# Mixture-of-experts rounds in a four-layer trunk: seven narrow rounds of 96 slots become alternating rounds of 96 and 64 slots, experts ranked by their token count

## What is computed

```python
def moe_ffn(h, router, w_gu, w_down):
    logits = (h @ router).astype(jnp.float32)
    top_v, top_i = lax.top_k(logits, TOP_K)                 # TOP_K = 2 of N_EXPERTS = 8
    w = jax.nn.softmax(top_v, axis=-1)
    combine = jnp.sum(jax.nn.one_hot(top_i, N_EXPERTS, dtype=jnp.float32) * w[..., None], axis=-2)
    gu = jnp.einsum('btd,edf->btef', h, w_gu)               # D_MODEL 1024 -> 2 * 1408
    g, u = jnp.split(gu, 2, axis=-1)
    act = jax.nn.silu(g) * u * combine[..., None].astype(h.dtype)
    return jnp.einsum('btef,efd->btd', act, w_down)         # 1408 -> 1024
```

## Time and profile before

| | us |
|---|---|
| median of three runs | 2552.91 (2550.69 to 2554.35) |
| the profiled execution, its own time | 2551.02 |
| its span, first to last instruction | 2549.2 |
| expert rounds of layer 1 in the trace | 808.8 to 1241.3 |
| expert rounds of layer 3 in the trace | 2092.3 to 2524.5 |

### The profile page before, as it was taken

How to read it: one execution, slowest core, us unless ns; L and a number is a source line. 1 busy time by engine, 2 the same in 40 slices (tenths; PEclk the granted TensorE clock), 3 DMA queues, 4 the chain that set the end, 5 groups by cost and what they waited for, 6 DMA issues and landing times.

```text
span 2549.2 us, 47861 instructions
## 1 busy us (share of the span) xinstructions
PE 2350.7 (92%) x21433; PEld 1688.1 (66%) x21433; DVE 477.5 (19%) x1366; ACT 400.2 (16%) x853; POOL 67.1 (3%) x111
## 2 busy tenths in 40 slices
PE   5998999999999999999798599999989899999997
PEld 3865667888887555445474478888868674555454
DVE  1324332000214000000202310002334331000001
ACT  1122232000101000000203320002133410000000
POOL 5000000000000000000100000000000000000000
PEclk7999999999999999999899589999989989999998
DMA  9758887543354999996668085413420069899971
GB/s 312 227 214 352 319 308 204 168 147 108 117 190 152 326 326 345 349 344 221 190 248 293 7 247 174 124 52 121 159 67 11 11 228 341 313 338 346 348 273 42
DMA packets 356876, 551.68 MB, mean 216 GB/s; under 512 B 11392, under 2 KB 311936, under 8 KB 344240
## 3 DMA queue, kind: packets, MB, share of 16 engines
q1 hardware_dynamic: 344208, 525.30, 59.4%
q0 software_dynamic: 5840, 17.72, 2.6%
q10 hardware_dynamic: 6688, 6.57, 0.8%
HBM read 537.24 MB, written 16.37 MB: 217 GB/s over the span
## 4 chain that ended last, share of the span: by engine, by line
PE 87%; DVE 5%; ACT 4%; DMA 3%; issue 1%; ACTq 0%; POOL 0%; SPq 0%; DVEq 0%; POOLq 0%
PE ps L626 84%; DMA ring<-in_ada_w 2%; ACT ring L1298 2%; ACT work L1298 1%; PE ps L1093 1%; PE ps L996 0%; DVE ring L1812 0%; DMA work<-y_rows,work 0%; DVE ring L1794 0%; DVE work L1675 0%; DVE ring L1817 0%; DVE ring L1947 0%; DVE ring L1802 0%; ACT hT L1298 0%; DMA y_rows<-work 0%
## 5 line engine op out<-in xcount | busy, mean ns | idle before, releaser
L626 PE MATMUL ps<-ring,work 128*32 128x256 f32 (+5 forms) x9576 | 790.4, 430 | 35.6 <-ACT work L1298 27.9
L626 PE MATMUL ps<-hT,ring 128*128 128x256 f32 x3200 | 706.0, 381 | 2.4 <-ACT hT L1298 2.1
L626 PEld LDWEIGHTS ps<-hT,ring 128*128 128x128 f32 x3200 | 608.0, 191 | 97.6 <-ACT work L1298 6.9
L626 PEld LDWEIGHTS ps<-ring,work 128*32 128x32 f32 (+2 forms) x9576 | 400.7, 114 | 400.5 <-issue 238.5
L1298 ACT ACTIVATE work<-ps 128x256 f32<-128x256 f32 (+4 forms) x276 | 115.0, 432 | 1475.8 <-PE ps L626 1280.6
L626 PE MATMUL ps<-work,ring 128*128 128x256 f32 (+1 forms) x1344 | 292.0, 377 | 10.5 <-DVE work L1879 5.9
L626 PEld LDWEIGHTS ps<-work,ring 128*128 128x128 f32 (+1 forms) x1344 | 244.6, 189 | 49.0 <-DVE work L1879 9.1
L626 PE MATMUL ps<-ring 64*64 64x64 f32 (+1 forms) x4192 | 185.0, 230 | 17.4 <-ACT ring L1298 7.2
L626 PEld LDWEIGHTS ps<-ring 64*64 64x64 f32 x4192 | 162.5, 139 | 57.0 <-ACT ring L1298 24.2
L1298 ACT ACTIVATE ring<-ps 128x512 f32<-128x512 f32 (+3 forms) x224 | 106.8, 483 | 349.4 <-PE ps L626 313.0
L626 PE MATMUL ps<-ring,csil 128*2 128x512 f32 x768 | 99.1, 606 | 20.1 <-DMA ring<-in_ada_w 19.8
(11 more groups left out here) (247 smaller groups left out, 990.8 us busy)
## 6 DMA issues: line engine op xcount, KB each, us to landing
ring<-in_moe_w_gu SPq DMA_DIRECT2D x96, 1536.0 KB, 9.7
ring<-in_ada_w SPq DMA_DIRECT2D x96, 1024.0 KB, 7.7
ring<-in_moe_w_down SPq DMA_DIRECT2D x48, 1536.0 KB, 11.0
ring<-in_ff_w_gu SPq DMA_DIRECT2D x88, 512.0 KB, 5.7
ring<-in_dn_w_in SPq DMA_DIRECT2D x32, 1024.0 KB, 5.5
ring<-in_moe_w_gu SPq DMA_DIRECT2D x32, 1024.0 KB, 5.5
ring<-in_ff_w_down SPq DMA_DIRECT2D x44, 512.0 KB, 6.9
ring<-in_moe_w_down SPq DMA_DIRECT2D x32, 512.0 KB, 6.2
```

What stands on the lines that cost most here:

```text
L626: return pe.matmul(out, lhsT, rhs, start=start, stop=stop, **kw)
```

## The change

Experts 1 to 7 are now sorted by their count on the chip. The three emptiest get rounds 1, 3 and 5, the next three rounds 2, 4 and 6, the fullest the wide round. Rounds 1, 3 and 5 have 64 slots and a body of their own, `small`, on PE, ACT and DVE. It pairs two blocks of 32 slots with two weight pieces: for one slice of the contraction the four tiles do block 0 and 1 of piece A and block 0 and 1 of piece B. Its gate and up part has 4 column sets of 8 groups, its down part 11 groups of four matmuls of 512 columns. There are two turns instead of three. The loop goes by twos, `small` and then `body`. Before a load into pieces 2 and 3 SP waits for the first down count as well. The count of 64 replaces 96 in the test for extra rounds of the experts in rounds 1, 3 and 5. At the start, `y_rows` is filled from slot 64 instead of 96 on for these three rounds. The core of the diff:

```diff
-CAP, BLK, GW, DW = 96, 32, 384, 256
+CAP, SMALL_CAP, BLK, GW, DW = 96, 64, 32, 384, 256
+ROUND_CAP = [CAP, SMALL_CAP, CAP, SMALL_CAP, CAP, SMALL_CAP, CAP] + [P] * (1 + EXTRA + 1)
...
@@ SP
                             if j in GU_FREE:
                                 sp.wait_ge(moe["p_gu"], (done[0] + r) * 6 + GU_FREE[j])
+                                if j in (GATE_D, UP_D):
+                                    sp.wait_ge(moe["p_dn"], (done[0] + r) * 4 + 1)
...
@@ POOL
-                r0 = CAP if x < NARROW else 0
+                r0 = ROUND_CAP[x] if x < NARROW else 0
                 po.dma_start(y_rows[P * x + r0:P * (x + 1), :], a["x_prompt"][0, r0:P]).then_inc(filled, 16)
...
@@ PE
+                def columns_small(q, pieces, bank, done):
+                    for j, _ in pieces:
+                        landed(q, j)
+                    for k in range(KC):
+                        for x, (j, width) in enumerate(pieces):
+                            for b in range(2):
+                                t = 2 * x + b
+                                ins = mm(ps[BLK * t:BLK * (t + 1), bank, 0:width], xg[:, k, BLK * b:BLK * (b + 1)],
+                                         weights(j, width)[:, k, :], k == 0, k == KC - 1)
+                    ins.then_inc(moe["p_gu"], done)
...
+                def down_small(q, s):
+                    pe.wait_ge(moe["a_at"], q * 3 + (1 + 2 * s))
+                    if s == 0:
+                        pe.wait_ge(moe["a_y"], q)
+                        pe.wait_ge(moe["d_y"], q)
+                        for j in (8, 9):
+                            landed(q, j)
+                    else:
+                        landed(q, 10)
+                    for c in (range(6, 11) if s else range(6)):
+                        w, n = down_rows(c), c - 6 * s
+                        for b in range(2):
+                            at = P * (n % 3) + 64 * (n // 3) + BLK * b
+                            for x in range(2):
+                                t = 2 * x + b
+                                ins = mm(ps[BLK * t:BLK * (t + 1), 4 + x, :], ma_T[:, s, at:at + BLK],
+                                         w[:, 512 * x:512 * x + 512], c == 0, c == 10, skip_group_check=True)
+                        if c in (2, 4, 7, 10):
+                            ins.then_inc(moe["p_dn"], 1)
+
+                def small(q):
+                    pe.wait_ge(moe["a_xg"], q + (i + 1))
+                    pe.wait_ge(moe["d_xg"], q + (i + 1))
+                    columns_small(q, ((GATE[0], GW), (GATE[1], GW)), PG[0], 1)
+                    columns_small(q, ((UP[0], GW), (UP[1], GW)), PU[0], 3)
+                    columns_small(q, ((GATE[2], GW), (GATE_D, DW)), PG[1], 1)
+                    columns_small(q, ((UP[2], GW), (UP_D, DW)), PU[1], 1)
+                    turn_small(q, 0)
+                    down_small(q, 0)
+                    pe.wait_ge(moe["d_act"], q * 3 + 3)
+                    pe.wait_ge(moe["d_g"], q + (i + 2))
+                    gather(0)
+                    gather(1)
+                    turn_small(q, 1)
+                    down_small(q, 1)
...
-                with pe.Fori(1, NARROW) as r:
-                    body(q0 + r, False)
+                with pe.Fori(1, NARROW, 2) as r:
+                    small(q0 + r)
+                    body(q0 + r + 1, False)
...
@@ DVE, overflow
-                link(dve.tensor_reduce(top_e, taken[:, 1:NE], AX.X, ALU.max))
...
+                link(tt(before_e[:, 0, :, 1:NE], taken[:, 0:NE, None].to_broadcast([P, NE, NARROW]),
+                        taken[:, None, 1:NE].to_broadcast([P, NE, NARROW]), ALU.is_gt))
+                link(dve.tensor_reduce(rank, before_e[:, 0, :, 1:NE], AX.X, ALU.add))
...
+                link(ts(where[:, 0:NE], rank, 2.0, 1.0, ALU.mult, ALU.add))
```

More of the change, by code:

```diff
@@ L235, in trunk @@
         raw, cand, where, taken = wk(8872, 2, NE), wk(8888, 2, CAND), wk(8936, CAND), wk(8960, CAND)
-        count, top_e, cap_e, is_top = wk(8984, NE), wk(8992, 1), wk(8993, NE), wk(9001, NE)
-        comb_c = wk(9009, 2, CAND)
+        count, cap_e, rank, high = wk(8984, NE), wk(8992, NE), wk(9060, NE), wk(9068, 2, NE)
+        comb_c = wk(9010, 2, CAND)
         iota = wk(9600, P)
@@ new lines, in turn_small @@
+                def turn_small(q, s):
+                    pe.wait_ge(moe["d_act"], q * 3 + (1 + 2 * s))
+                    if s == 1:
+                        pe.wait_ge(moe["a_at"], q * 3 + 1)
+                    for c in range(2 if s else 3):
+                        ins = pe.transpose(ps[:, 6, c * P:(c + 1) * P], ma_s[:, s, c * P:(c + 1) * P], ident)
+                    if s == 1:
+                        ins = pe.transpose(ps[:, 6, 2 * P:2 * P + 64], ma_s[0:64, s, 2 * P:3 * P], ident[0:64, 0:64])
+                    ins.then_inc(moe["p_tr"], 1 + s)
@@ L1523, in store, with output_small, store_small, small @@
                             .then_inc(moe["y_out"], 16)
+                def output_small(q):
+                    act.wait_ge(moe["p_dn"], q * 4 + 4)
+                    act.wait_ge(moe["y_out"], q * 64 + 64)
+                    f(y_m[0:64, :], ps[0:64, 4, :], ACT.Copy).then_inc(moe["a_y"], 1)
+                def store_small(q, r):
+                    act.wait_ge(moe["a_y"], q + 1)
+                    act.wait_ge(moe["d_y"], q + 1)
+                    for x in range(4):
+                        act.dma_start(y_rows[bass.ds(r * P, 64), QUARTER * x:QUARTER * (x + 1)],
+                                      y_m[64 * (x // 2):64 * (x // 2) + 64, QUARTER * (x % 2):QUARTER * (x % 2 + 1)]) \
+                            .then_inc(moe["y_out"], 16)
+                def small(r):
+                    q = q0 + r
+                    output(q - 1)
+                    act.wait_ge(moe["p_gu"], q * 6 + 1)
+                    act.wait_ge(moe["d_act"], q * 3)
+                    f(mg_s, ps[:, PG[0], 0:GW], ACT.Silu).then_inc(moe["a_silu"], 1)
+                    store(q - 1, r - 1)
+                    act.wait_ge(moe["p_gu"], q * 6 + 5)
+                    act.wait_ge(moe["d_act"], q * 3 + 1)
+                    f(mg_s[0:64, DW:GW], ps[0:64, PG[1], DW:GW], ACT.Silu)
+                    f(mg_s[:, 0:DW], ps[:, PG[1], 0:DW], ACT.Silu).then_inc(moe["a_silu"], 2)
+                    act.wait_ge(moe["p_tr"], q * 3 + 1)
+                    act.wait_ge(moe["p_dn"], q * 4)
+                    f(ma_T[:, 0, :], ps[:, 6, 0:GW], ACT.Copy).then_inc(moe["a_at"], 1)
+                    tokens(q + 1)
+                    act.wait_ge(moe["p_tr"], q * 3 + 3)
+                    f(ma_T[:, 1, 0:2 * P + 64], ps[:, 6, 0:2 * P + 64], ACT.Copy).then_inc(moe["a_at"], 2)
                 def body(r, first):
@@ L1578, in experts @@
                 body(0, True)
-                with act.Fori(1, NARROW) as r:
-                    body(r, False)
+                with act.Fori(1, NARROW, 2) as r:
+                    small(r)
+                    body(r + 1, False)
                 output(q0 + NARROW - 1)
@@ L2007, in overflow @@
                 link(stt(taken[:, 0:NE], count, float(NE), es, ALU.mult, ALU.subtract))
-                link(dve.tensor_reduce(top_e, taken[:, 1:NE], AX.X, ALU.max))
[L2009 to L2018, removed]
+                link(tt(before_e[:, 0, :, 1:NE], taken[:, 0:NE, None].to_broadcast([P, NE, NARROW]),
+                        taken[:, None, 1:NE].to_broadcast([P, NE, NARROW]), ALU.is_gt))
+                link(dve.tensor_reduce(rank, before_e[:, 0, :, 1:NE], AX.X, ALU.add))
+                ts(high[:, 0], rank, 2.5, None, ALU.is_gt)
+                ts(high[:, 1], rank, 5.5, None, ALU.is_gt)
+                link(ts(where[:, 0:NE], rank, 2.0, 1.0, ALU.mult, ALU.add))
+                link(stt(where[:, 0:NE], high[:, 0], -5.0, where[:, 0:NE], ALU.mult, ALU.add))
+                link(tt(where[:, 0:NE], where[:, 0:NE], high[:, 1], ALU.subtract))
+                link(tt(cap_e, high[:, 0], high[:, 1], ALU.add))
+                link(ts(cap_e, cap_e, float(CAP - SMALL_CAP), float(SMALL_CAP), ALU.mult, ALU.add))
+                dve.memset(where[:, 0:1], 0.0)
+                link(dve.memset(cap_e[:, 0:1], float(CAP)))
                 link(tt(count, count, cap_e, ALU.subtract))
@@ L2059, in chosen_rows @@
             def chosen_rows(l):
[L2061 to L2064, removed]
+                ts(col_v, slotv, -0.5, None, ALU.is_gt)
+                link(tt(col_w, slotv, cst[:, None, C_RCAP:C_RCAP + COLS].to_broadcast([P, 2, COLS]), ALU.is_lt))
                 link(tt(col_w, col_w, col_v, ALU.mult))
@@ L2131, in gated, with output_small, small @@
                     tt(ma_s[:, s, 0:DW], mg_s[:, 0:DW], ps[:, PU[s], 0:DW], ALU.mult).then_inc(moe["d_act"], 1)
+                def output_small(q):
+                    dve.wait_ge(moe["p_dn"], q * 4 + 4)
+                    dve.wait_ge(moe["y_out"], q * 64 + 64)
+                    cp(y_m[64:P, :], ps[64:P, 5, :]).then_inc(moe["d_y"], 1)
+                def small(r):
```

(18 more changed lines are left out.)

15 lines of the change are left out of this document (9 added, 6 removed).

## The result

The changed kernel takes 2506.1 us (median of 4 runs, 2505.7 to 2512.2) against 2552.7 (4 runs): a ratio of 0.9827, 95% interval 0.9812 to 0.9842. That is 46.6 us faster, where 84.5 were forecast, and 12 us above the range.

The account below looks back on a forecast made before the run. TensorE was taken to bound the kernel, DMA close behind. -96.6 (small rounds) + 2 x (4.0 wait + 1.5 clock) + 1.1 (fill) = -84.5 us, giving a forecast of 2468 us, range 2460 to 2478.

Parts of the forecast that it names:

- What bounds it: Expert rounds: TensorE bounds them, a narrow round needing 52.5 us of TensorE and 46.4 us of DMA.
- The price of a small round: Rounds 1, 3 and 5: each takes 36.4 us of TensorE, 16.1 us less than a narrow round.
- the 0.858 from the wide round: Small round's down part: a group of four tiles with 512 columns costs 0.858 us, the wide round's price per matmul.
- The step that failed: Three small rounds in each of two layers: 96.6 us less in all, if weights never come late.
- the rivals: Other outcomes: DMA binds harder 0.19, no wait 0.12, overlap worse 0.08, clock falls 0.06, a round more 0.02.
- something unseen: Chance left for the gain being lost in something the prediction did not see: 0.01.
- The waits for weights: Head of round 6: TensorE waits 4.0 us a layer for piece 2; no wait in rounds 1 to 5.
- The price of a piece: Weight loads: each of an expert's 11 pieces takes 4.22 us of DMA.
- The clock: After the wait for weights: half of a 3 us clock dip, 1.5 us more a layer.
- The fill of `y_rows`: At the start: the fill grows by 3 x 128 KB, 1.1 us more.
- The count of rounds: Rounds stay eight, one wide round a layer; the rival of a further round had chance 0.02, 2588 us.

Follow-up runs that it names:

- 1396: Instructions in TensorE's loop in the kernel before the change, which took 2552.7 us.
- 1552: Changed kernel with the small body in all of rounds 1 to 6, two in each pass of TensorE's loop: 2449.9 us.
- 1692: Changed kernel with slices 1 to 5 of each gate and up product left out in the looped narrow bodies: 2450.1 us.
- 1884: Changed kernel with slices 1 to 3 of each gate and up product left out in the looped narrow bodies: 2457.1 us.
- 1788: Changed kernel with slices 1 to 4 of each gate and up product left out in the looped narrow bodies: 2455.2 us.

## Why the prediction was wrong

- **What bounds it, right.** TensorE did, with DMA 6 us a narrow round behind, and some 3 us slower than TensorE in a pair with a small round (92.1 against 88.9).
- **The price of a small round, right.** In layer 1 a pair of small and narrow rounds takes 88.9 us (857.84 to 946.77, from one start of the last down part to the next but one); less the narrow round's 52.5 that is 36.4, as forecast. The six down slices of four tiles with 512 columns stand as 5.36 us, 0.89 each with the start of the stretch, so the 0.858 from the wide round was a fair price. 96.6 us of TensorE's work did go.
- **The step that failed** is the sentence under that sum, that three small rounds in each of two layers are 96.6 us less, if weights never come late. It made late weights the only way to lose them. The loop by twos was in my own list of what changes, and I priced its products and waits but not the jump back. TensorE's loop became larger than what is held near the engine, and each of the four jumps costs 11.7 to 12.5 us: gaps, and a low clock after them. It was none of the rivals; I had left 0.01 for something unseen. The trace of before could not show it, as nothing in it jumps back over so much code. The Trainium skill could have: "Runtime: NRT & Kernel Launch", under "Instruction fetch mechanics", says that a taken branch whose target isn't in the current window of two pages forces a fetch of the target page before execution can go on. That such a fetch stops the engine, the runs agree with. The sizes they don't bear out. Two pages of 256 instructions would have stopped the loops of 1396 and 1552 too. The 2048 instructions that the section gives TensorE would have held those of 1692 to 1884, where here the limit was near 1700.
- **The waits for weights, right, but hidden.** In the changed kernel none appears, because the gaps give the loads 24 us a layer to catch up. Without the gaps they are there, 6.1 us a layer where 4.0 were worked out: 4.1 at the head of round 6 for 4.0, and 2.0 at round 4, where I had none. The price of a piece was 4.19 us for 4.22.
- **The clock, right in size by luck** for a wait of 4 us. I had taken half of the dip in the earlier trace rows and called the whole one 3 us. But its 3 us at the low level are not lost whole: by the windows there the dip costs 2 x (0.02 + 0.50 + 0.34) = 1.7 us. After the wait of 4.12 us the whole dip came, 2.5 x (0.32 + 0.36) = 1.7 us, and after the waits of 2.0 and 1.8 us none. After the gaps it cost more, 2.5 and 3.4 us.
- **The fill of `y_rows`, 1.1 us, not tested.** Round 0 of layer 1 began between 808.1 and 816.4 in the profiled executions, with and without it, which is more than the term.
- **The count of rounds, right.** One wide round a layer.

The sum repaired: -96.6 + 48.4 (gaps and clock at four heads) + 0 (waits, covered) + 1.1 = -47.1, and 46.6 were measured.

## What to carry to other kernels

A loop on TensorE has a size, and float32 matmuls count four instructions each. Before joining bodies under one loop, add them up. By the estimate of seven blocks of 256, a loop of up to some 1530 instructions is held wherever it begins, one of over 1792 never is, and between them it depends on where it begins. Above some 1530 write the loop out, which cost nothing here, or keep it short. Where two resources are close, as PE and DMA here, place the light rounds so that the slower one has caught up before each; and look at what a gap covers: the waits for weights showed only once it was gone.

## What the hardware showed that I had not expected

A jump back over a loop of 1788 instructions or more stopped TensorE for 5.1 to 6.4 us, in layer 1 always with a second stop of 3.6 to 4.3 us seven records later; one over 1552 or fewer did not stop it, and at 1692 it did in layer 1 alone. With about half of the weight bytes the two stops were 3.65 and 1.42 us, the second of them with the DMA engines idle. How much of the first is the fetch's own stays open. So does whether the border is exactly seven blocks of 256; the places of the second stop and the two layers at 1692 say so, but no run tested it alone.

As priced, and still worth knowing: a group of four column tiles that reads two weight pieces, or 512 columns a tile, costs what one matmul of its widest tile costs. The stretch with 32 groups of 384 columns took 27.31 us in a small round and 27.32 in a narrow one, and six slices of 512 columns took 5.36 us for 5.42 on the whole array.
